# Pauses between the phases of small jobs, spread of the modulation weights and small-table loads in a two-block transformer kernel

## The reference

```python
h = rms_norm(x, ln1)
qkv_a, beta_a, decay_a, z_a, qkv_b, gate_a, gate_b = split_columns(h @ w_in)
y_a = gated_deltanet(qkv_a, beta_a, decay_a, z_a, ...) @ w_branch_a   # 8 heads of 128
y_b = moba_attention(rope(q_b), rope(k_b), v_b) @ w_branch_b          # 8 heads of 128
x = x + (sigmoid(gate_a) * y_a + sigmoid(gate_b) * y_b) @ w_out
u_gate, u_val = split(causal_dwconv(rms_norm(x, ln2) @ w_up))
x = x + (silu(u_gate) * u_val) @ w_down
x = rms_norm(x, final_norm)
```

```python
shift, scale, gate = split(silu(c) @ w_mod[l] + b_mod[l])             # w_mod: 2048 x 6144
h = rmsnorm(x, norm_gain[l]) * (1 + scale) + shift
q_a, k_a, v_a, g_a, q_i, k_i, w_i, q_b, k_b, v_b, g_b = split(h @ w_in[l])
y_a = sparse_attention(..., rel_bias) * silu(g_a)                     # index, top 64, bias by t5 bucket
y_b = head_groupnorm(retention(rotary(q_b), rotary(k_b), v_b)) * silu(g_b)
x = x + gate * (concat(y_a, y_b) @ w_out[l])
```

## Time and profile before

| | us |
|---|---|
| median of three runs | 2092.43 |
| lowest and highest | 2089.18, 2105.43 |
| the profiled execution, its own time | 2096.29 |
| its span, first to last instruction | 2094.5 |

### The profile page before, as it was taken

One profiled execution on the slowest core, in us unless ns is written; L12 is line 12 of the kernel. 1 busy time (PEld: TensorE's weight loads), 2 busy tenths in 40 slices (PEclk: granted clock), 3 DMA queues, 4 the chain that ended last, 5 costly groups with the idle time before them and its releaser, 6 DMA issues. The chain is left out here.

```text
span 2094.5 us, 34021 instructions
## 1 busy us (share of the span) xinstructions
PE 1921.8 (92%) x13292; PEld 1788.7 (85%) x13292; DVE 1711.1 (82%) x2198; ACT 1240.4 (59%) x1921; POOL 270.4 (13%) x182
## 2 busy tenths in 40 slices
PE   5998899899999997999899987999989879999798
PEld 5787889899998897989889976998878669988797
DVE  6777777875998898988898986789879876887787
ACT  5456644645566765556666658446666574566664
POOL 0000040031010012221100100132101002221020
PEclk8998899899999998999999998899999988999999
DMA  7785565865999777689889976868689867686885
GB/s 233 236 284 181 191 191 182 293 201 183 353 354 357 238 255 240 227 297 297 296 293 334 317 263 195 268 187 267 223 280 316 307 201 245 203 272 198 282 309 203
DMA packets 270764, 536.88 MB, mean 256 GB/s; under 512 B 31880, under 2 KB 40973, under 8 KB 269581
## 3 DMA queue, kind: packets, MB, share of 16 engines
q1 hardware_dynamic: 270317, 532.62, 75.9%
q10 hardware_dynamic: 288, 2.10, 0.3%
HBM read 532.55 MB, written 2.10 MB: 255 GB/s over the span
## 5 line engine op out<-in xcount | busy, mean ns | idle before, releaser
L150 PE MATMUL ps<-hh_r,w 128*128 128x256 f32 x3384 | 866.8, 295 | 43.6 <-DVE ring_r L1821 23.0
L150 PEld LDWEIGHTS ps<-hh_r,w 128*128 128x128 f32 x3384 | 674.2, 199 | 57.5 <-DVE ring_r L1821 27.7
L150 PE MATMUL ps<-hlo,ring_r 128*128 128x256 f32 x2816 | 707.8, 290 | 0.0
L1821 DVE SCALAR_TENSOR_TENSOR ring_r<-ring,w 128x1024 fp32r<-128x1024 f32 x449 | 555.7, 1254 | 165.0 <-ACT w L1370 162.3
L1370 ACT ACTIVATE w<-ring 128x1024 fp32r<-128x1024 f32 x449 | 465.2, 1052 | 209.8 <-DMA ring<-in_w_in 94.0
L150 PEld LDWEIGHTS ps<-hlo,ring_r 128*128 128x128 f32 x2816 | 561.4, 199 | 1.0 <-issue 0.7
L150 PE MATMUL ps<-hlo,AR_r 128*128 128x256 f32 x1104 | 268.0, 283 | 0.0
L1821 DVE SCALAR_TENSOR_TENSOR AR_r<-AR,w 128x1024 fp32r<-128x1024 f32 x172 | 214.5, 1262 | 46.0 <-ACT w L1370 45.1
L150 PE MATMUL ps<-w,AR_r 128*128 128x512 f32 x584 | 233.7, 400 | 8.7 <-DVE AR_r L1821 7.9
L1370 ACT ACTIVATE w<-AR 128x1024 fp32r<-128x1024 f32 x172 | 178.9, 1056 | 66.6 <-DMA AR<-in_w_in 23.4
L150 PEld LDWEIGHTS ps<-hlo,AR_r 128*128 128x128 f32 x1104 | 213.0, 193 | 0.3 <-issue 0.2
(11 more groups left out here) (204 smaller groups left out, 2765.5 us busy)
## 6 DMA issues: line engine op xcount, KB each, us to landing
ring<-in_w_in SPq DMA_DIRECT2D x285, 512.0 KB, 5.2
ring<-in_w_mod SPq DMA_DIRECT2D x131, 512.0 KB, 5.5
ring<-in_w_up SPq DMA_DIRECT2D x115, 512.0 KB, 5.5
AR<-in_w_in SPq DMA_DIRECT2D x83, 512.0 KB, 5.7
ring<-in_w_out SPq DMA_DIRECT2D x63, 512.0 KB, 6.5
ring<-in_w_down SPq DMA_DIRECT2D x63, 512.0 KB, 5.9
AR<-in_w_up SPq DMA_DIRECT2D x61, 512.0 KB, 5.5
AR<-in_w_mod SPq DMA_DIRECT2D x48, 512.0 KB, 6.1
```

The source lines that it names most:

```text
L150: return e.matmul(o, l, x, start=start, stop=stop, skip_group_check=True)
L1821: return e.scalar_tensor_tensor(o, a, s, b, op0, op1)
```

## The change

It touches the plan alone; every product, copy and DMA of before is still made, once.

- Pauses: `convq`, `convk` give their PE sum 4 steps after the square instead of 3; `gdn` has two steps instead of one between phases 5 to 19; `bias` units take 7 steps instead of 6, with 4 instead of 3 between DVE's table and PE's product, and the first comes 2 steps after the start instead of 6; `sparse` phase 5 comes 3 steps after 4 instead of 2; `retain` phase 1 comes 3 after 0 instead of 2, and its transposes (phase 5) 5 after 4 instead of 3.
- `moba` pairs 0 and 1 start at product chunk 24 instead of 48, pairs 2 and 3 at 48 instead of behind them.
- `gdn` pairs 0 and 1 start 6 steps later behind an empty job, `rest`.
- The 17 small DMAs go out in six portions over phases of a new job `biasin`, which starts one product block pair (16 chunks) ahead of `bias`. POOL's memsets go with it.
- The `early` modulation chunks are placed anew: 42 instead of 52 before `yb` (chunk 145), 9 in the 16 chunks of `yb` and 8 in the 48 of `ga`/`ya` instead of 12 over both, 8 instead of 6 in `resid`, 45 instead of 42 in `up`.

```diff
--- before.py
+++ after.py
@@ -158,11 +158,11 @@
 
 PAUSES = {
     "xpose": (6, 1, 1), "setup": (2, 1, 1, 1, 1), "rope": (0, 2, 1), "moba": (1, 1, 1, 4, 2, 1, 1),
-    "bd": (0, 3, 1), "convq": (0, 1, 1, 3, 2, 1), "convk": (0, 1, 1, 3, 2, 1), "convv": (0, 1, 1),
-    "z": (0, 1), "gdn": (2, 1, 1, 1, 2) + 14 * (1,) + (1, 1, 1, 1, 1, 4, 1, 1), "merge": (0, 0, 1, 1),
-    "upg": (0, 1, 1), "upv": (0, 1, 1), "bias": (6,) + 12 * (2, 3, 1), "rope2": (12, 1), "modend": (3,),
+    "bd": (0, 3, 1), "convq": (0, 1, 1, 4, 2, 1), "convk": (0, 1, 1, 4, 2, 1), "rest": (6,), "convv": (0, 1, 1),
+    "z": (0, 1), "gdn": (2, 1, 1, 1, 2) + 14 * (2,) + (1, 1, 1, 1, 1, 4, 1, 1), "merge": (0, 0, 1, 1),
+    "upg": (0, 1, 1), "upv": (0, 1, 1), "biasin": (3, 1, 1, 1, 1, 1), "bias": (2,) + 12 * (2, 4, 1), "rope2": (12, 1), "modend": (3,),
     "scalex": 8 * (1,), "indexer": 13 * (1,), "kn": (0, 3, 2, 1), "qn": (0, 1, 2, 1),
-    "sparse": (1, 1, 1, 4, 2, 1), "rot": (0, 1), "retain": (2, 2, 2, 1, 3, 1, 1), "glu": (0, 1, 1),
+    "sparse": (1, 1, 1, 4, 3, 1), "rot": (0, 1), "retain": (3, 2, 2, 1, 5, 1, 1), "glu": (0, 1, 1),
 }
 
 USES = {
@@ -655,10 +655,11 @@
         return lambda: [enqueue(queue, [j]) for j in jobs]
 
     for blk in range(2):
-        add(W1, 4112 + 512 * blk, 512, KT, "CM", "h0", "rope", ("mq", blk), None if blk else [first_norm], fresh=not blk)
+        add(W1, 4112 + 512 * blk, 512, KT, "CM", "h0", "rope", ("mq", blk),
+            [launch(Job("moba", 0)), launch(Job("moba", 1))] if blk else [first_norm], fresh=not blk)
         add(W1, 5136 + 512 * blk, 512, KT, "CM", "h0", "rope", ("mk", blk))
         add(W1, 6160 + 512 * blk, 512, KT, "TM", "h0", "mv", (blk,))
-    add(W1, 3072, 16, KT, "TM", "h0", "bd", (), [launch(*[Job("moba", hp) for hp in range(4)])])
+    add(W1, 3072, 16, KT, "TM", "h0", "bd", (), [launch(Job("moba", 2)), launch(Job("moba", 3))])
 
     def qkv(blk):
         for kind, c0 in (("q", 0), ("k", 1024), ("v", 2048)):
@@ -687,7 +688,7 @@
     qkv(0)
     for blk in range(2):
         b_z1 = add(W1, 3088 + 512 * blk, 512, KT, "TM", "h0", "z", (blk,),
-                   [lend_gk0] if blk else [launch(Job("gdn", 0), Job("gdn", 1))])
+                   [lend_gk0] if blk else [lambda: [enqueue(queue, [Job("rest"), Job("gdn", bt)]) for bt in range(2)]])
     qkv(1)
     b_gb = [add(W1, 9232 + 512 * blk, 512, KT, "CM", "h0", "gb", (blk,),
                 [launch(Job("gdn", 2), Job("gdn", 3))] if blk == 1 else None) for blk in range(4)]
@@ -706,6 +707,9 @@
         inline("rstd", 1)
         norm()
 
+    def load_bias():
+        enqueue(short, [Job("biasin")])
+
     def start_bias():
         enqueue(queue, [Job("bias")])
         enqueue(queue, [Job("rope2")])
@@ -713,7 +717,7 @@
     b_up = []
     for j in range(11):
         b_up.append(add(t["w_up"][0], 512 * j, 512, KT, "CM", "h1", "up", (0, j),
-                        [ffn_need] if j == 0 else [start_bias] if j == 2 else None, fresh=j == 0))
+                        [ffn_need] if j == 0 else [load_bias] if j == 1 else [start_bias] if j == 2 else None, fresh=j == 0))
         b_up.append(add(t["w_up"][0], DFF + 512 * j, 512, KT, "CM", "h1", "up", (1, j)))
         if (4 * j + 4) % FH == 0:
             for blk in range(4):
@@ -812,8 +816,9 @@
     z1, gb0, yb0, res0, up0 = (first_chunk(b) for b in (b_z1, b_gb[0], b_yb[0], b_res, b_up[0]))
     early = [c for L in range(2) for b in range(4) for c in add_mod(L, b)]
     puts = []
-    for lo, hi, n in ((24, 48, 10), (50, z1, 11), (z1, z1 + 16, 6), (z1 + 16, gb0, 11), (gb0, yb0, 14), (yb0, res0, 12),
-                      (res0, up0 - 4, 6), (up0 + 16, marks[0] - 16, 42)):
+    ga0 = yb0 + 16
+    for lo, hi, n in ((24, 48, 8), (50, z1, 8), (z1, z1 + 16, 4), (z1 + 16, gb0, 8), (gb0, yb0, 14), (yb0, ga0, 9), (ga0, res0, 8),
+                      (res0, up0 - 4, 8), (up0 + 16, marks[0] - 16, 45)):
         puts += spread(early[:n], (lo, hi))
         early = early[n:]
     for L in range(2):
@@ -978,19 +983,25 @@
             e.wait_ge(*normed(2 + L))
             e.dma_start(GB, t["b_mod_2"][L, 4096:6144].partition_broadcast(128)).then_inc(*in_gate[L].step("row"))
 
-        def bias(J, seg):
-            if seg == 0:
-                pos2 = t["positions_2"].rearrange("a s -> (a s)")
+        def bias_in(J, seg):
+
+            pos2 = t["positions_2"].rearrange("a s -> (a s)")
+            if seg == 1:
                 e.wait_ge(*bias_pool.after("zero"))
                 e.dma_start(PQR, pos2.partition_broadcast(128)).then_inc(*in_bias.step("pos"))
-                for g in range(4):
+            if 1 <= seg <= 4:
+                g = seg - 1
+                pp = slice(32 * g, 32 * g + 32)
+                e.dma_start(RBP[pp, :], t["rel_bias_2"]).then_inc(*in_bias.step("p", g))
+                e.dma_start(RBM[32 * g + 1:32 * g + 32, :], t["rel_bias_2"][0:31, :]).then_inc(*in_bias.step("m", g))
+            if seg >= 5:
+                for g in (2 * seg - 10, 2 * seg - 9):
                     pp = slice(32 * g, 32 * g + 32)
-                    e.dma_start(RBP[pp, :], t["rel_bias_2"]).then_inc(*in_bias.step("p", g))
-                    e.dma_start(RBM[32 * g + 1:32 * g + 32, :], t["rel_bias_2"][0:31, :]).then_inc(*in_bias.step("m", g))
                     for kb in range(2):
                         e.dma_start(PKC[pp, 32 * kb:32 * kb + 32],
                                     pos2[128 * kb + 32 * g:128 * kb + 32 * g + 32].partition_broadcast(32)
                                     ).then_inc(*in_bias.step("k", g, kb))
+            if seg == 6:
                 in_bias.at[("all",)] = in_bias.n
 
         def oevac(J, seg):
@@ -1006,7 +1017,7 @@
             load_vec(vec[name], src, in_vec0, name)
         in_vec0.at[("all",)] = in_vec0.n
         e.dma_start(X[:, 1, :], t["x"][0, 128:256, :]).then_inc(*in_x[1].step("x"))
-        parts = {"loads": loads, "final": final, "decay": decay_mask, "gate": gate, "bias": bias, "oevac": oevac}
+        parts = {"loads": loads, "final": final, "decay": decay_mask, "gate": gate, "biasin": bias_in, "oevac": oevac}
         for what, *a in steps:
             if what == "send":
                 send(*a)
@@ -2444,11 +2455,13 @@
                 e.wait_ge(*up_dve.after("silu", 0, j, hf))
                 tt(z, z, flat2(SG[:, 2 * hf:2 * hf + 2, :]), MUL).then_inc(*up_pool.step("mul", *J.at))
 
-        def bias(J, seg):
+        def bias_in(J, seg):
             if seg == 0:
                 e.wait_ge(*normed(1))
                 e.memset(RBM, 0.0)
                 e.memset(RBW, 0.0).then_inc(*bias_pool.step("zero"))
+
+        def bias(J, seg):
             if seg % 3 == 1 and seg < 37:
                 i = seg // 3
                 qt, kb = ((0, 0), (1, 0), (1, 1))[i // 4]
@@ -2502,7 +2515,7 @@
                    MUL).then_inc(*glu_pool.step("y", *J.at))
 
         parts = {"gdn": gdn, "merge": merge, "upv": up,
-                 "bias": bias, "indexer": indexer, "kn": kn, "sparse": sparse, "rot": rot, "glu": glu}
+                 "biasin": bias_in, "bias": bias, "indexer": indexer, "kn": kn, "sparse": sparse, "rot": rot, "glu": glu}
         for what, *a in steps:
             if what == "phase" and a[0].kind in parts:
                 parts[a[0].kind](*a)
```

## The result

| | before | after |
|---|---|---|
| median, us | 2094.76 (4 runs) | 2067.70 (4 runs) |
| lowest and highest | 2089.18, 2105.43 | 2064.41, 2069.30 |
| span of the profiled execution | 2094.5 | 2067.5 |

The changed kernel takes 0.9875 of the time of before, 95% interval 0.9839 to 0.9910: 27 us less. (The four runs of before are the three known ahead and one more.) The forecast was 62 us less. The time lies at the upper edge of the stated range (2005 to 2068) and the sign is right, but less than half of the forecast gain came.

A forecast was written before the change was run, and what follows sets the result against it. PE bounds the kernel, losing time by idling and at the lower clock. Savings by place summed to 70.8 us, less 9 for unplaced waits: 62, giving 2032.5 span, 2034 in all and a 2031 us median; range 2005 to 2068.

The forecast's parts named there:

- the prediction's formula: Loss of a stretch: PE's idle time plus (1 - PEclk) times its length; said to count a little too much.
- the sum 1.9 + 1.3 + 7: Ahead of `convk`: one more step, one addition less and some 60 small `gdn` products exceed the 7.4 us wait.
- The 2 us for `moba`'s new place: Chunks 24 to 48: a new wait of 2 us as two `moba` pairs come in; 4 at worst, none at best.
- the 2 us that were set down: Chunks 96 to 209: `finish_jobs` takes `gdn`'s phase 25 at 169 instead of 171, counted as -2 us.
- The rival of the ports: POOL's instructions in `gdn` hold up DVE's: 82 us if each of 50 does, 2112 us; chance 0.04.
- 8, 13 and 10 us: Savings forecast for `sparse` and `retain` in the first layer, the same in the second layer, and `bias`.
- -2 in `up`: Three modulation chunks more in `up`: cost 3.8 us at most, none at least, counted as -2.
- the waits move: Most places: DVE is the limit, time comes back at the next split; 30 us won, 2062 us; chance 0.22.
- my own numbers in front: Savings: 18 and 8.8 us in chunks 48 to 80, -2 in 24 to 48, 20 - 1 - 2 in 96 to 209.
- The 9 us that I took off: Whole kernel: 9 us off the 70.8 us sum, since some remaining waits of 2 to 3 us drop the clock.
- all goes: Six stretches: everything lost but `bd`'s 5 and 30 us for splits is saved, less 10 overcounted; 1988 us; chance 0.08.
- rise to 45: Sign of being right: PE's waits for splits go up from 33.3 to about 45 us.

The follow-up runs named there:

- e8: Kernel of e1 with the modulation chunks placed as before the change: 2067.0 us, ratio 0.9882.
- e12: Changed kernel with `moba` launched as before (pairs 0 and 1 at chunk 49, pairs 2 and 3 at 61): 2075.9 us, ratio 0.9915.
- e3: Changed kernel with `gdn`'s pauses of 1 as before and without the empty job `rest`: 2092.8 us, ratio 0.9991.
- e5: Kernel before with only `gdn`'s pauses of 2 and `rest` added, slot GK0 lent at chunk 89: 2070.1 us, ratio 0.9892.
- e1: Changed kernel with slot GK0 lent to the weights one block later, at product chunk 89 instead of 81: 2064.8 us, ratio 0.9862.
- e2: Changed kernel with the pauses of `sparse` and `retain` as before: 2070.7 us, ratio 0.9888.
- e4: Changed kernel with the `bias` job and its 17 small DMAs as before: 2067.4 us, ratio 0.9878.
- e9: Kernel of e1 with `bias`, its small DMAs and the pauses of `sparse` and `retain` as before: 2066.8 us, ratio 0.9879.
- e10: Kernel of e1 with `retain` phase 1 five steps after phase 0 instead of three, transposes four after phase 4 instead of five: 2059.8 us, ratio 0.9850.
- e11: Kernel of e1 with 42 instead of 45 modulation chunks in `up` and 12 instead of 9 in `yb`: 2065.3 us, ratio 0.9874.

## Why the prediction was right and wrong

**What was right.** The stretch of chunks 48 to 80 takes 92.0 us, forecast 95, before 130.7. By the prediction's formula it gained 26.2 us, forecast 26.8, by the finer reading 22.2. Chunks 96 to 112 gained 18.4 by the formula, forecast 20, by the finer reading 16.4. In the first of the two, spread (e8) and the early pairs (e12) both have a part. The wait ahead of `convk` went, as the sum 1.9 + 1.3 + 7 said: PE has 80 small products between chunks 105 and 111 where it had 16, some 60 more as forecast. e3 and e5 show which of the three terms carried it: `gdn`'s products, for in e3, with the step and the thinner modulation but without them, chunks 96 to 112 lose 13.8 us, and in e5, with them alone, 1.9. The 2 us for `moba`'s new place did not come (chunks 16 to 48 lose 0.5 us), and chunks 160 to 208, where `finish_jobs` stands, lose about the 2 us that were set down. The rival of the ports took nothing that shows: the additions of `yb` have a median of 1.278 us and one of 2.194, and `yb` loses nothing, though single splits beside `bias` on POOL last 2.9 us.

**The step that was missing: the queue of SP.** The prediction moved `gdn`'s phase 4 from chunk 79 to 85 and looked at PE, DVE and POOL. It did not ask who else waits for that phase. The slot is lent at chunk 81, between the two numbers, and SP waits in order. That is 9.6 us lost in chunks 80 to 96, forecast at nothing, for the sum has no term for it. e1 shows the cause; of its price 5.9 us can still be seen at chunk 208 and 3 in the medians.

**The step that was mis-sized: retain, sparse and bias.** 8, 13 and 10 us were set down, with -2 in `up`: 29 in all, and this is the larger part of what is missing. Measured is 1459.7 against 1460.1 from chunk 208 on, and e2, e4 and e9, each without one part or all, agree. The steps that a phase gets more did what was said of them: the waits for `stg` of L1813 went from 16.4 to 0.4, and the wait of 8.8 ahead of `bias` to 3.7. The error is in what follows. Two kinds of return are seen. A job with longer pauses moves its later phases and the jobs behind it, and these meet what they did not meet before: `retain` pair 3 meets a `glu` block, and 20.1 us of waits stand ahead of phase 1 instead of 9.5. The prediction had looked at pair 3 and asked only whether it ends ahead of the `glu` that reads it. e2 shows that the pauses bring these waits; that the `glu` block is behind them is read from the timeline of the longest one alone. And with a wait gone, PE comes sooner to the next split or transpose; e10 shows that for some 16 of 21 us. The prediction had the second kind as its first rival, "the waits move", with 0.22 and 2062, and it named the sign against it, 33.3 us of waits for splits.

That rival should have been applied by place, and the rows say how, though not by DVE's busy share of a stretch alone: that was 83.84 of 91 us, 184.17 of 216 and 146.21 of 177 where nothing came, but also 50.91 of 59 us in chunks 96 to 112, where nearly all came. What differs is what lay beside: ahead of chunks 96 to 112 stood a stretch in which PE was full and DVE busy 46.15 of 67 us, and the change moved `gdn`'s products of PE from there to where PE waited (PE's records go from 510 to 372 in the one and from 331 to 464 in the other). Taken over chunks 48 to 112, DVE was busy 190 us beside 229 of PE's. Behind chunk 208 the change moved inputs and products of the same jobs by a few steps, and DVE's work beside PE's stayed as it was. This reading fits the runs; none was made to test it.

With 0 behind chunk 208 and my own numbers in front the sum is 42, and with the slot's 10 it is 32 for 27 measured. The 9 us that I took off for waits I could not place are not in these sums; with them the sum is 23. By the finer reading the parts meet the measured time: 22.2 in chunks 48 to 80 and 16.4 in 96 to 112, less 9.6 for the slot and 2 in chunks 160 to 208, are 27.0, for 26.6 at chunk 208. The formula's double count, of which the prediction warned and which it priced (at 10) only in the rival "all goes", had put the losses of these two stretches at 37.9 and 23.6 instead of 34.3 and 19.4.

**Of the signs named.** "No wait over 4 us ahead of `macc`, `convk`, `gdn` or `bias`" fell with 4.8 ahead of `gdn` phase 5 and 5.0 ahead of `bias`. The waits for splits did not rise to 45; they are 31.0. Small DMAs in portions: so it is, from 722.8 to 734.3 us, and e4 shows no worth in it.

**What stays open.** The time behind chunk 208 differs between kernels whose plans there are alike or nearly so: 1463.4 us in e1, 1459.7 in the changed kernel, 1448.7 in e8. One profiled execution of each can't tell a cause from scatter. Of the differences between e8 and e1 behind chunk 208, e11 has one, 42 chunks in `up`, and takes 1455.7; the rest of the 14.7 us was not tried.

## What to carry to other kernels

- When a phase is delayed, list all who wait for its event: engines, buffers and slots that are lent out on it. A slot lent before its release stands in the plan blocks the whole DMA queue, since sends go in order; the lending has to move along.
- Cover for a late product is worth its time where it moves work of the waiting engine from a full stretch to the one with the wait (20 us from `gdn` alone). Where a longer pause only shifts input and product of one job, and the late engine has as much to do around it as before, the pause mostly names another place for the wait: in e10, of 21 us of waits taken away 5 are left in the medians, and even these are not sure.
- A busy share over one stretch does not tell these two cases apart; look at the stretches beside it, too.
- A denser spread of side work and the work that covers it belong together. Here, with `gdn` beside them nine additions in 16 chunks cost nothing, without it 13.5 us, and twelve cost 4.8 even with it (one profiled execution of each).
